# A hybrid attention, convolution and expert layer: the convolution taps of one channel block go from GpSimd to the end of VectorE's list

## The reference, cut to what matters

```python
h = rms_norm(x, attn_norm_g)
q, k, v, cv, cg = split(h @ w_in)
attn = blocked_attention(rope(q), rope(k), v)        # 8 heads, 2 kv heads, head size 64
u = cv * sigmoid(cg)                                 # 512 channels
conv = silu(layer_norm(depthwise_conv(u, 31 taps) + dw_b))
x = x + concat(rms_norm(attn), rms_norm(conv)) @ w_out
x = x + expert_choice_ffn(rms_norm(x, ffn_norm_g))   # 16 experts
```

## Time and profile before

| | |
|---|---|
| median of three runs | 2694.64 us (2694.27 to 2696.27) |
| the profiled execution | 2694.56 us |
| its span in the trace | 2692.6 us |
| mean granted clock of PE | 0.982 |
| busy share of the span | PE 95%, DVE 69%, ACT 52%, POOL 15% |
| chain that ended last | PE 88%, DVE 5%, ACT 3% |

### The profile page before, as it was taken

How to read it: one execution, slowest core, us unless ns; L and a number is a source line. 1 busy time by engine, 2 the same in 40 slices (tenths; PEclk the granted TensorE clock), 3 DMA queues, 4 the chain that set the end, 5 groups by cost and what they waited for, 6 DMA issues and landing times.

```text
span 2692.6 us, 39956 instructions
## 1 busy us (share of the span) xinstructions
PE 2560.6 (95%) x15886; PEld 2348.1 (87%) x15886; DVE 1853.9 (69%) x2177; ACT 1394.9 (52%) x1687; POOL 393.3 (15%) x326
## 2 busy tenths in 40 slices
PE   6999799997897799999999999999999999999997
PEld 5888689986786789899898998989989899899996
DVE  5787899986348667676676666766667666676664
ACT  4224555666322456555465555655556555565563
POOL 2644791000000101011010110101101001010010
PEclk9999999998997899999999999999999999999999
DMA  4122000002233667677687777768868778677773
GB/s 151 35 63 79 16 1 1 1 1 95 94 112 131 196 225 249 221 259 245 228 254 227 242 250 231 251 221 260 245 224 256 229 239 255 226 253 225 247 237 117
DMA packets 348093, 477.37 MB, mean 177 GB/s; under 512 B 10000, under 2 KB 301200, under 8 KB 347792
## 3 DMA queue, kind: packets, MB, share of 16 engines
q1 hardware_dynamic: 340880, 449.74, 51.4%
q0 software_dynamic: 7040, 25.17, 3.8%
HBM read 449.71 MB, written 25.17 MB: 176 GB/s over the span
## 4 chain that ended last, share of the span: by engine, by line
PE 88%; DVE 5%; ACT 3%; issue 1%; DMA 1%; POOL 1%; SPq 0%; ACTq 0%; POOLq 0%; DVEq 0%
PE psum L1560 30%; PE psum L1562 14%; PE psum L1313 8%; PE psum L1314 8%; PE psum L1315 8%; PE psum L1429 5%; PE psum L1582 4%; PE psum L1583 4%; PE psum L1416 2%; PE psum L1404 2%; DVE conv L881 1%; ACT probs L654 1%; DVE top L1131 1%; DVE aff L1134 1%; DVE topi L1133 1%
## 5 line engine op out<-in xcount | busy, mean ns | idle before, releaser
L1220 DVE TENSOR_TENSOR w_lo<-raw,w_hi 128x2048 fp32r<-128x2048 f32 x384 | 880.2, 2293 | 494.6 <-ACT w_hi L763 492.8
L1560 PE MATMUL psum<-xgT,w_hi 128*128 128x384 f32 x4096 | 1170.3, 360 | 2.4 <-issue 2.4
L1562 PE MATMUL psum<-xgT,w_lo 128*128 128x192 f32 x4096 | 1026.9, 251 | 0.0
L763 ACT CAST w_hi<-raw 128x2048 fp32r<-128x2048 f32 x384 | 733.4, 1910 | 332.8 <-PE psum L1583 332.8
L1562 PEld LDWEIGHTS psum<-xgT,w_lo 128*128 128x128 f32 x4096 | 784.0, 191 | 0.6
L1560 PEld LDWEIGHTS psum<-xgT,w_hi 128*128 128x128 f32 x4096 | 770.5, 188 | 3.5 <-issue 2.8
L539 POOL DMA_INDIRECT out_dram<-o_p,put_p x16 | 25.7, 1606 | 1543.8 <-ACT o_s L810 1472.8
L881 DVE SCALAR_TENSOR_TENSOR conv<-conv,colp 128x1024 f32<-128x1024 f32 (+1 forms) x210 | 236.8, 1127 | 4.0
L1313 PE MATMUL psum<-w_hi,hid_st 128*128 128x512 f32 x512 | 212.9, 416 | 0.0
L1314 PE MATMUL psum<-w_lo,hid_st 128*128 128x512 f32 x512 | 202.5, 396 | 0.0
L1315 PE MATMUL psum<-w_hi,hid_st 128*128 128x512 f32 x512 | 202.4, 395 | 0.0
(11 more groups left out here) (200 smaller groups left out, 3511.8 us busy)
## 6 DMA issues: line engine op xcount, KB each, us to landing
raw<-in_w_gate_dram SPq DMA_DIRECT2D x128, 1024.0 KB, 5.3
raw<-in_w_up_dram SPq DMA_DIRECT2D x128, 1024.0 KB
raw<-in_w_down_dram SPq DMA_DIRECT2D x128, 1024.0 KB, 5.0
wi_raw<-in_w_in_dram SPq DMA_DIRECT2D x56, 256.0 KB, 3.7
out_dram<-x SPq DMA_DIRECT2D x12, 512.0 KB, 2.6
h_rows<-h SPq DMA_DIRECT2D x12, 512.0 KB, 2.9
xin<-in_x_prompt_dram SPq DMA_DIRECT2D x8, 512.0 KB, 3.4
wo_raw<-in_w_out_dram SPq DMA_DIRECT2D x8, 512.0 KB, 6.4
```

Of the source, the lines that this page charges most:

```text
L763: act.copy(w_hi[:, j % SPLIT_SLOTS, :], raw[:, j % RAW_SLOTS, :]).then_inc(e_hi, 1)
L1220: dve.tensor_tensor(w_lo[:, j % SPLIT_SLOTS, :], raw[:, j % RAW_SLOTS, :], w_hi[:, j % SPLIT_SLOTS, :].bitcast(F32), ALU.subtract).then_in ...
L1560: pe.matmul(bank[:, 0:2 * CAP], w_hi[:, slot, w0:w0 + P], xgT[:, half, k, :], start=(k == 0), stop=False, skip_group_check=True)
L1562: last = pe.matmul(bank[:, 0:CAP], w_lo[:, slot, w0:w0 + P], xgT[:, half, k, 0:CAP], start=False, stop=(k == KD - 1), skip_group_check=True)
```

## The change

POOL's taps and their buffer and semaphores are gone. DVE's list has all 248 taps, the sample's block 0 ahead of its blocks 1 to 3. Units 64 to 77 do one tap each, and unit 78 does all that are left. The convolution transposes of a prompt tile wait for the 124 prompt taps alone, those of a sample tile for all 248.

```diff
-                tapped = in_region(ra, "tapped", [P, N_SAMPLE], F32)
...
-        TAPS = [(0, c, k) for c in range(NC_CONV) for k in range(CONV_K)] + [(1, c, k) for c in (1, 2, 3) for k in range(CONV_K)]
-        POOL_TAPS = [(1, 0, k) for k in range(CONV_K)]
+        TAPS = [(0, c, k) for c in range(NC_CONV) for k in range(CONV_K)] + [(1, c, k) for c in range(NC_CONV) for k in range(CONV_K)]
+
+        PROMPT_TAPS = NC_CONV * CONV_K
...
-            for w, (g, c, k) in enumerate(POOL_TAPS):
-                out, u, tap = conv_operands(g, c, k)
-                if w:
-                    pool.wait_ge(pool_tap, w)
-                if k == 0:
-                    pool.wait_ge(glu_u, glu_no[g, c, 0] + 1)
-                    pool.tensor_scalar(out, u, tap, colp[:, COL_BIAS + c:COL_BIAS + c + 1], ALU.mult, ALU.add
-                                       ).then_inc(pool_tap, 1)
-                else:
-                    pool.tensor_scalar(tapped[:, :], u, tap, None, ALU.mult).then_inc(pool_mul, 1)
-                    pool.wait_ge(pool_mul, w)
-                    pool.tensor_tensor(out, out, tapped[:, :], ALU.add).then_inc(pool_tap, 1)
...
-                        if g == 1:
-                            dve.wait_ge(pool_tap, len(POOL_TAPS))
...
                 if u < PROMPT_UNITS:
                     conv_run(3 - (u % 4 == 0) if sample_next else 2 - u % 2)
+                elif u < PROMPT_UNITS + 2 * ROT_TILES - 2:
+                    conv_run(1)
                 else:
                     conv_run(len(TAPS))
...
-                pe.wait_ge(conv_tap, len(TAPS))
-                pe.wait_ge(pool_tap, len(POOL_TAPS))
+                pe.wait_ge(conv_tap, PROMPT_TAPS if g == 0 else len(TAPS))
```

More of the change, by code:

```diff
@@ L230, in encoder_layer_kernel @@
         t_rstd = sem("t_rstd"); t_norm = sem("t_norm"); rope_a = sem("rope_a"); rope_b = sem("rope_b"); rope_c = sem("rope_c")
-        v_ok = sem("v_ok"); conv_tap = sem("conv_tap"); pool_tap = sem("pool_tap"); pool_mul = sem("pool_mul")
+        v_ok = sem("v_ok"); conv_tap = sem("conv_tap");
         qk_hi = sem("qk_hi"); qk_lo = sem("qk_lo"); qk_T = sem("qk_T"); q_st_ok = sem("q_st_ok"); k_st_ok = sem("k_st_ok")
```

## The result

The changed kernel takes 2699.72 us in the median of 20 runs (2697.95 to 2703.01), the kernel before 2694.39 us in 20 runs beside them. The ratio is 1.0021, with a 95% interval of 1.0014 to 1.0027: slower by 5.3 us by the medians and by 3.8 to 7.3 us by the interval, where 5.3 was forecast. The profiled execution took 2699.3 us.

The account below looks back on a forecast made before the run. PE bounded clean prompt units, DVE those beside POOL's taps, a two-engine round the sample's units. Gains 2.6 + 8.4 = 11.0, costs 1.1 + 4.0 + 10.1 + 1.1 = 16.3: 5.3 us slower, 2699.9 us, range 2695.0 to 2705.5.

Parts of the forecast that it names:

- Part one: Turning stage: without POOL's taps, three longer DVE pieces of the chain shrink, gaining 2.6 us (bounds 0 and 2.6).
- part two: Prompt units 1 to 22: without POOL's taps they run at the clean pace, gaining 8.4 us (bounds 7 and 8.5).
- a lock for a whole instruction: Prompt taps beside POOL: two lose 0.91 us, not a whole instruction of 1.5 us, so the rows agree only in part.
- Part three: Units 62 to 78: 31 more DVE taps cost 1.1 us at 62 to 64, 4.0 at even units, 10.1 at unit 78.
- Rival (b): Sample units: ACT and PE set the round, DVE's idle time swallows taps, only 2.5 us overflow; 2686 us, chance 0.06.
- Part four: After unit 78's stall: PE's clock falls to its lower level, costing 1.1 us (bounds 0 and 2).
- the rest of the round is DVE's: Round after unit 78's stall: only PE's output and scores, 1.43 us, are priced at the low clock, giving 1.1 us.
- Part five: Convolution transposes of prompt tiles 0 to 7: waiting for 124 taps, done by unit 28, changes nothing.
- Rival (a): Sample units: clock or round recovers late, some 3 us a round, or odd taps cost 4.6; 2704 to 2706, chance 0.10.
- the cover of the odd units: Odd units 65 to 77: a 0.66 us tap fits DVE's 0.8 us idle half; uncovered, up to 4.6 us.
- Rival (c): Turning stage and prompt units: POOL's taps did not slow DVE, so gain is 0; 2711 us, chance 0.04.
- The forecast's own range: Whole kernel: 2.5 to 8 us slower, from bounds of the clock, units 62 to 64 and the gains.

Follow-up runs that it names:

- The memset run: The kernel before with POOL's 61 instructions for the sample's block 0 replaced by 200 memsets of 128x512 into the same buffer: 2682.71 us, ratio 0.9954.

## Why the prediction was right

**Part one and two, POOL's taps removed.** Forecast 2.6 and 8.4 us, measured 2.59 and 8.56. In part two the step that carried it was to set one stretch with POOL against a stretch of the same work without it. In part one the three longer pieces of the chain were the whole difference; that it came out within 0.01 us is luck, since this stage moves by 0.8 us with the moment at which the clock comes back. The remark that the rows bear out a lock for a whole instruction only in part misread them: who comes second waits for the rest of the instruction under way, which was 0.83 us of POOL's 1.56 at 348.14, and so the loss of 0.91 us is what such a lock would give.

**Part three, 31 taps on DVE.** The prices came true: even units 3.89 us against 4.0, odd units 0 (shown free by the run with odd units alone), the 13 taps 10.12 against 10.1, units 22 to 64 0.95 against 1.1. The model behind them was right for the changed kernel and not quite for the one before. There the chain that ended last passes PE and ACT in nearly all of these rounds, and not DVE; in the changed kernel it passes DVE:

```profile
583.72 1.13 PE psum L1429 x8
584.84 0.46 PE psum L1404 x2
585.30 0.44 PE psum L1443 x4
585.74 0.45 PE psum L1416 x4
...
586.75 0.79 ACT probs L654 x2
```
```profile
583.75 0.66 DVE conv L866
584.41 0.62 DVE bst L996
```

Before, DVE's scaling is only ready at the same moment: it ends at 588.09, 0.15 us ahead of the output at 588.24, and PE's transposes ahead of that output, which start at 587.59, end at 588.24 as well. Two paths of 4.53 us ended together. That the even taps cost all of their length rests on this tie, which the prediction did not see: a DVE path shorter by some tenths would have taken them off each tap. Rival (b), in which DVE's idle time swallows taps and PE and ACT set the round, had the chain right and the price wrong. It fell with the changed kernel's rounds of 5.19 us and with the run without the 13.

**Part four, the clock.** The clock fell as forecast, and the size was off: 1.78 us against 1.1. The step that was mis-sized was "the rest of the round is DVE's": I priced one output and the scores at the low clock. But behind them on PE come the convolution's transposes and those of the probabilities, and the chain passes all four pieces:

```profile
611.66 2.05 PE psum L1416 x8
613.71 0.85 PE psum L1391 x2
614.57 0.85 PE psum L1429 x4
615.42 0.65 PE psum L1403 x4
```

The same four take 1.13 + 0.46 + 0.44 + 0.45 = 2.48 us in the chain of the kernel before, shown above. At 0.78 of their length more they would have been priced at 1.93. From the output of unit 78 to that of unit 79 it takes 615.89 - 611.66 = 4.23 us in PE's timeline, against 613.48 - 611.17 = 2.31 in the run that kept PE busy, so 1.92 more; in the half round behind it 0.16 is won back. The term is inside its bounds of 0 to 2.

**Part five, the wait of prompt tiles.** Nothing, as forecast: PE's timeline shows no wait at a convolution transpose of units 64 to 78.

Rival (a) did not come: the clock was back within the first round, and the cover of the odd units held. Rival (c) fell with the run without block 0. The forecast's sum was closer than its terms deserve: the clock's 0.7 us too little stands against some 0.5 us too much in the others, the rest of the launch moved by more than that between two executions, and the difference of the medians is known to about 2 us either way. The forecast's own range of 2.5 to 8 us does not follow from the bounds beside it: they give 5.3 - 1.1 - 0.6 = 3.6 to 5.3 + 0.9 + 0.9 + 2 = 9.1. The measured 5.3 lies in both.

## What to carry to other kernels

In a round that passes from engine to engine, ask of each place in an engine's order whether it lies between two hand-overs or in the wait beside them: here a tap cost nothing in the half in which DVE had been idle, and one more in the other half its full length. Where two paths end together, as here before the change, either of them can set the price. Work that was left over at a deadline cost its whole length and the clock after it (10.1 and 1.8 us here), so spread it over the idle halves first. When one engine's work slows another's, compare a stretch with it and one without it, and share the work so that only what finds cover is moved.

## What the runs showed of the hardware

DVE's taps, which read two SBUF operands, were slowed by POOL's taps (3.51 us for two) and not by POOL's writing (2.60 us beside an unbroken run of memsets). It goes both ways: POOL's sums took up to 2.35 us in place of 1.26.

Behind a tap of the sample, the next tap, which waits for its result, starts 0.79 us later (12 such steps and one of 0.66 make the 10.13 us of unit 78); an instruction that does not need the result starts 0.66 us later (568.11 to 568.77 in the changed kernel). The wait for DVE's own result had a price of 0.13 us.

Late in attention all ten traces have an idle stretch of PE of 2.07 to 2.08 us. In the trace of the changed kernel the granted clock stayed at 1.00 behind it, in that of the kernel with 11 POOL taps it fell:

```profile
642.00:645.00 3.00, 1.56 (x13) 1.56 (x14) 1.59 (x4) 2.19 (x5) 0.00 (x0) 1.00 0.00 0
645.00:648.00 3.00, 2.88 (x20) 2.03 (x20) 2.44 (x6) 1.72 (x5) 0.00 (x0) 1.00 0.00 0
```
```profile
631.00:634.00 3.00, 1.73 (x13) 1.71 (x14) 1.47 (x5) 2.19 (x5) 0.00 (x0) 0.94 0.00 0
634.00:637.00 3.00, 3.00 (x15) 2.67 (x13) 1.66 (x4) 1.54 (x5) 0.00 (x0) 0.50 0.00 0
```

From one table load of ACT to the next around it, 12.01 us passed in the first (641.31 to 653.32) and 13.08 in the second (630.14 to 643.22). The memset run (13.08) and the one without the 13 taps (13.32) are like the second, all others like the first. So an idle stretch of the same length was followed by a loss of 1.1 to 1.3 us or by none, which is as much as some of the terms above; why the clock fell in some and not in others stays open.
